# The keys' product of a recurrence level moved from VectorE to GpSimd

## The reference, cut to what matters

```python
log_f = jnp.logaddexp(jnp.log(lbf), jnp.log1p(-lbf) + jax.nn.log_sigmoid(f_logit))
k = -jnp.expm1(log_f)
bc = jnp.cumsum(log_f)                       # within a chunk
decay = jnp.exp(where(causal, diff of bc, -inf))
A = jnp.einsum('bhtk,bhsk,bhtsk->bhts', qx, kx, decay)
o_intra = A @ v;  o_inter = (q * exp(bc)) @ S
S_new = exp(b_last) * S + (k * exp(b_last - b)).T @ v
```

## Time and profile before

| | |
|---|---|
| median of 3 runs | 4003.78 us |
| the profiled execution's own time | 3998.87 us |
| its span | 3997.0 us |
| TensorE busy | 3660.4 us (92%) |
| VectorE busy | 2068.4 us (52%) |
| GpSimd busy | 1398.6 us (35%) |
| ScalarE busy | 863.5 us (22%) |
| mean granted clock of TensorE | 0.955 |

### The profile page before, as it was taken

How to read it: one execution, slowest core, us unless ns; L and a number is a source line. 1 busy time by engine, 2 the same in 40 slices (tenths; PEclk the granted TensorE clock), 3 DMA queues, 4 the chain that set the end, 5 groups by cost and what they waited for, 6 DMA issues and landing times. The chain is left out here.

```text
span 3997.0 us, 45908 instructions
## 1 busy us (share of the span) xinstructions
PE 3660.4 (92%) x18494; PEld 2943.3 (74%) x18494; DVE 2068.4 (52%) x3162; ACT 863.5 (22%) x1690; POOL 1398.6 (35%) x602
## 2 busy tenths in 40 slices
PE   7897878999999989978999799899999888899998
PEld 3683457888887879956888566788888566788886
DVE  5796453223337556674233367864243377853342
ACT  3213412110002243311100244431000343422001
POOL 2321034225555200005456222235445322245454
PEclk9998889999999999988999899999999899999999
DMA  5443312221113100013332131123332221123332
GB/s 169 148 148 138 121 42 64 64 64 58 53 40 98 53 14 1 2 63 94 96 100 90 54 85 49 48 62 101 96 95 79 74 67 48 53 79 92 98 93 76
DMA packets 400351, 306.81 MB, mean 77 GB/s; under 512 B 11228, under 2 KB 367782, under 8 KB 399559
## 3 DMA queue, kind: packets, MB, share of 16 engines
q1 hardware_dynamic: 398040, 303.37, 25.1%
q10 hardware_dynamic: 2095, 0.44, 0.1%
HBM read 297.48 MB, written 6.29 MB: 76 GB/s over the span
## 5 line engine op out<-in xcount | busy, mean ns | idle before, releaser
L422 POOL TENSOR_TENSOR low<-raw,high 128x1024 fp32r<-128x1024 f32 (+1 forms) x437 | 1060.6, 2427 | 1495.4 <-DVE high L346 1495.4
L487 PE MATMUL scores<-high 128*128 128x512 f32 (+1 forms) x1944 | 741.3, 381 | 85.4 <-POOL low L422 63.7
L487 PE MATMUL scores<-low,high 128*128 128x512 f32 (+1 forms) x1944 | 728.6, 375 | 0.0
L487 PE MATMUL scores<-high,low 128*128 128x512 f32 (+1 forms) x1944 | 726.6, 374 | 0.0
L346 DVE CAST high<-raw 128x1024 fp32r<-128x1024 f32 (+1 forms) x437 | 399.6, 915 | 501.7 <-PE scores L487 272.1
L487 PE MATMUL bank<-high 128*128 128x512 f32 (+1 forms) x1480 | 541.5, 366 | 0.2
L487 PE MATMUL bank<-low,high 128*128 128x512 f32 (+1 forms) x1480 | 538.8, 364 | 0.0
L487 PE MATMUL bank<-high,low 128*128 128x512 f32 (+1 forms) x1480 | 538.1, 364 | 0.0
L487 PEld LDWEIGHTS scores<-high 128*128 128x128 f32 x1944 | 377.2, 194 | 163.8 <-POOL low L422 68.0
L487 PEld LDWEIGHTS scores<-high,low 128*128 128x128 f32 x1944 | 375.1, 193 | 65.6
L487 PEld LDWEIGHTS scores<-low,high 128*128 128x128 f32 x1944 | 376.5, 194 | 62.5 <-issue 1.0
(11 more groups left out here) (628 smaller groups left out, 5396.0 us busy)
## 6 DMA issues: line engine op xcount, KB each, us to landing
raw<-in_mlp_w SPq DMA_DIRECT2D x128, 512.0 KB, 3.9
raw<-in_w_in SPq DMA_DIRECT2D x76, 512.0 KB, 3.9
ring<-in_ada_w SPq DMA_DIRECT2D x32, 1024.0 KB, 7.3
raw<-in_w_gate SPq DMA_DIRECT2D x44, 512.0 KB, 3.8
raw<-in_w_up SPq DMA_DIRECT2D x44, 512.0 KB, 3.8
raw<-in_w_down SPq DMA_DIRECT2D x40, 512.0 KB, 3.4
mix<-in_ada_w SPq DMA_DIRECT2D x16, 1024.0 KB, 7.0
raw<-in_od_w_in SPq DMA_DIRECT2D x29, 512.0 KB, 3.9
```

What stands on the lines that cost most here:

```text
L422: pool.tensor_tensor(tile(low, u), tile(raw, u), tile(high, u).bitcast(F32), ALU.subtract)\
L487: mm = pe.matmul(out(p), stationary, moving, start=(k0 + k == 0 and i == 0), stop=(k0 + k == job.kc - 1 and i == len(pairs) - 1))
```

## The change

The keys' product of each level is formed by GpSimd, after it has subtracted the weights of unit u+2 and before it goes on to unit u+1. It reads and writes the same tiles and raises the same semaphore; on GpSimd it waits for the pairing of three levels earlier and for the exponential.

```diff
@@ HgrnLevels.gpsimd @@
         if u == self.first - 1:
             pool.wait_ge(self.attention.kept, MH)
             pool.memset(self.attn, 0.0).then_inc(self.cleared, 1)
+        for a in self.at(u + 1):
+            hd, lv = self.units[a]
+            if lv < LEVELS:
+                if a >= self.RING:
+                    pool.wait_ge(self.paired, a - self.RING + 1)
+                pool.wait_ge(self.raised, self.decayed(a))
+                pool.tensor_tensor(self.ring(self.ke, a), self.k[:, hd, :], self.ring(self.e, a), ALU.mult)\
+                    .then_inc(self.keys_decayed, 1)
@@ HgrnLevels.vector @@
                 dve.wait_ge(self.raised, self.decayed(a))
                 dve.tensor_tensor(self.ring(self.qe, a), self.q[:, hd, :], self.ring(self.e, a), ALU.mult)\
                     .then_inc(self.queries_decayed, 1)
-                dve.tensor_tensor(self.ring(self.ke, a), self.k[:, hd, :], self.ring(self.e, a), ALU.mult)\
-                    .then_inc(self.keys_decayed, 1)
```

## The result

The changed kernel took 4024.18 us (median of 5 runs, 4019.0 to 4029.31) against 4001.8 us (median of 5, 4000.95 to 4003.97) for the kernel before: 1.0053 times as long, 95% interval 1.0038 to 1.0067. It is 22.4 us slower; 21.8 us and 4025 us had been forecast.

The account below looks back on a forecast made before the run. VectorE's loop was taken to bound the levels' stage; trip terms summed to 10.9 us per layer, 21.8 us for two, giving 4025 us from a median of 4003.8, range 4008 to 4040.

Parts of the forecast that it names:

- Who sets the stage: Levels' stage of either layer: VectorE's loop sets the pace, working or waiting 135.9 of 141.1 us; TensorE follows.
- The plain trip: VectorE's loop: cast done at T + 3.90 to 3.98, not T + 3.01 (T: first exponential ready); 0.9 us per trip.
- The price of a key that waited: GpSimd's keys' product after waiting for VectorE: 1.18 us in place of 1.26.
- Unit 31: Trip with the cumulated sum, which could be held up differently: left at 0.9 us, between 0.6 and 0.9.
- Units 33 and 34: GpSimd runs `low` and `ya_low` before unit 33's keys, delaying the next subtractions and products: 1.5 us for both trips.
- Unit 35: VectorE afterwards waits 3.5 us for ScalarE's gate function, which does not depend on the keys: 0 us.
- Unit 36: VectorE's 0.5 us of wait for TensorE is there to be used up: 0.4 us.
- The signs: Profile after: one query per trip 1.3 us or more, longer casts, GpSimd some 95 us busier, stage about 152 us.
- That the engines run side by side: Rival: GpSimd's multiply does not exclude VectorE's, about 10 trips per layer gain 0.6 us, 3992 us; 7%.
- That it is hidden: Rival: TensorE sets the pace and VectorE's waits have slack, so no change, 4004 us; 10%.
- The costlier rival: Rival: TensorE's clock falls more often or each handover costs, 31 us and more, 4035 to 4042 us; 13%.
- The 115 ns: Skill's figure for a blocked engine's restart; at four handovers, 0.46 us per trip, estimate 4035 us; not used.

Follow-up runs that it names:

- the run of the memsets: Changed kernel with the keys' product left out and GpSimd writing zeros twice into each key tile instead, same waits: 3996.1 us, stage 137.9 us.

## Why the prediction was right, point by point

The starts of the first query of each trip, read off VectorE's timeline of both kernels (first layer), give the price of every trip:

```
unit            29    30    31    32    33+34  35    36    37    38    39    40    41    42    sum
before       10.62 11.64 12.24  7.52  20.81  12.62  9.20 10.28  7.80  7.53  8.73  8.76 10.32
changed      11.61 12.55 12.84  8.47  22.36  12.62 10.09 11.28  8.72  8.52  9.64  9.74 11.31
difference    0.99  0.91  0.60  0.95   1.55   0     0.89  1.00  0.92  0.99  0.91  0.98  0.99  11.7
forecast      0.9   0.9   0.9   0.9    1.5    0     0.4   0.9   0.9   0.9   0.9   0.9   0.9   10.9
```

(The last is to the first step of the states. The columns of this table are trips as VectorE runs them; 34's query is left out, since it meets a key in the changed kernel.)

*Who sets the stage.* VectorE's loop: shown by the run without keys, in which 12 of the 14 trips get shorter when VectorE loses two products in each, nine of them by the products' own 0.6 us.

*The plain trip.* 0.96 us as a mean of nine (29, 30, 32 and 37 to 42) for 0.9. The order of the handovers came out as written, the first query, a key, the second query, a key, the cast. The price of a key that waited, 1.18 us, was near (T + 2.31 for T + 2.25 when the cast is issued).

*Unit 31.* I named 0.6 to 0.9 and took 0.9; it was 0.60. Before, VectorE's line 3212 started late, 0.44 us of it for ScalarE, and GpSimd's `low` had gone ahead of it at 2526.43; the cumulated sum then ran undisturbed. In the changed kernel line 3212 no longer waits, goes ahead of `low` (from 2537.58), and the sum is held in its place, which is cheaper: after the end of `low` VectorE has one instruction left in place of two. Before, then changed:

```profile
2526.79 2.55 DVE L3212 SCALAR_TENSOR_TENSOR x_all<-b,x_all 128x512 f32<-128x512 f32 x1 [0.44 <-ACT x_all L3225]
2529.38 1.22 DVE L3214 TENSOR_TENSOR_SCAN b<-restart,x_all 128x512 f32<-128x512 f32 x1
...
2537.42 0.68 DVE L3212 SCALAR_TENSOR_TENSOR x_all<-b,x_all 128x512 f32<-128x512 f32 x1
2538.14 3.27 DVE L3214 TENSOR_TENSOR_SCAN b<-restart,x_all 128x512 f32<-128x512 f32 x1
```

In the changed kernel all eight of these sums are held:

```profile
L3214 DVE TENSOR_TENSOR_SCAN b<-restart,x_all x8: 3273/3286/3307, 2401.2 to 3422.9; 128x512 f32<-128x512 f32 x8
```

*Units 33 and 34.* 1.55 us for 1.5. VectorE's and GpSimd's timelines show the walk: both queries undisturbed, the cast at T + 4.2 held until GpSimd's `ya_low` is through, GpSimd's two keys and `low` after it, and the two subtractions and the two queries stretched between them.

```profile
2554.77 0.69 DVE L3333 TENSOR_TENSOR work<-q,work 128x512 f32<-128x512 f32 x1 [0.83 <-ACT work L3355]
2555.96 0.69 DVE L3333 TENSOR_TENSOR work<-q,work 128x512 f32<-128x512 f32 x1 [0.49 <-ACT work L3355]
...
2558.96 2.83 DVE L346 CAST high<-raw 128x1024 fp32r<-128x1024 f32 x1
...
2564.00 3.47 DVE L3324 TENSOR_TENSOR work<-b 128x512 f32<-128x512 f32 x2
2567.39 3.49 DVE L3333 TENSOR_TENSOR work<-q,work 128x512 f32<-128x512 f32 x2
```
```profile
2557.87 3.38 POOL L370 TENSOR_TENSOR ya_low<-ya,ya_high 128x1024 fp32r<-128x1024 f32 x1 [5.07 <-DVE ya_high L359]
2561.21 2.94 POOL L3297 TENSOR_TENSOR work<-f,work 128x512 f32<-128x512 f32 x2
2564.11 2.81 POOL L422 TENSOR_TENSOR low<-raw,high 128x1024 fp32r<-128x1024 f32 x1
```

*Unit 35.* 0 for 0: the wait for ScalarE's gate function shrank from 3.5 to 2.5 us and took it all in.

*Unit 36.* The term mis-sized most: 0.89 for 0.4. I counted VectorE's 0.5 us of wait for TensorE as there to be used up. But TensorE's product in that unit took 7.3 us in place of 6.4, at the lower of its two clock levels for longer, so the wait was still 0.4 us. The first of its 24 products start some 0.43 us apart, the later ones 0.23, and the slow stretch lasts 3.1 us in place of 1.4. The granted clock over that product, before and after, in the columns of the earlier trace rows:

```profile
2574.10:2580.60 6.50, 6.50 (x29) 5.36 (x28) 3.94 (x7) 5.43 (x14) 0.97 (x1) 0.88 0.00 1
```
```profile
2587.40:2594.80 7.40, 7.40 (x29) 6.04 (x28) 4.45 (x5) 5.44 (x14) 4.37 (x3) 0.76 0.00 0
```

In the second layer the same trip went from 9.29 to 9.73 us, 0.44, which is what I had counted on; that is the difference between the layers' 11.7 and 11.2. The slack is there, then, but it is TensorE's, and its clock moves it.

*The terms together.* Nine plain trips +0.5, unit 31 -0.3, 33 and 34 +0.05, unit 36 +0.5: 11.7 for 10.9 in the first layer. With the second layer's 11.2 that is 22.9 us; the medians differ by 22.4, against the 21.8 forecast. The errors partly cancel, but the largest is 0.5 us.

*The signs.* The stage came to 151.85 us for "about 152", the cast, where it stands directly behind the queries, to 1.75 us and more for "1.5 us and more", GpSimd's busy time to 95.4 us more over both layers for "some 95", its products to 1.73 us as a mean for 1.8. One sign was missed in size: the second query of a trip lasts 1.20 us, not 1.3 or more. Its record begins only with the second exponential, at T + 1.19, and ends at T + 2.4.

*The rivals.* That the engines run side by side fell with the plain trip and with the run of the memsets, which is what side by side looks like. That it is hidden fell with the stage. The costlier rival did not happen: TensorE's mean clock in the stage did fall, to 0.91, but in the trips above that shows only as 0.5 us in one trip of one layer.

*The 115 ns.* The Trainium skill ("SBUF — State Buffer", section "A bandwidth-pool intuition that's wrong (but worth ruling out)") gives "blocked until DVE-end + ~115 ns" for a DMA whose descriptors GpSimd has to write. Carried over to the four handovers of a trip, as the prediction's estimate by that page did, it would make a plain trip cost 0.90 + 0.46 = 1.4 us. It cost 0.96; the traces here show no such addition between compute instructions.

## What to carry to other kernels

When an instruction is moved from VectorE to GpSimd, add up how long the two engines exclude each other, not how long each is busy: here 1.2 us of VectorE's time per trip was traded for 2.4 us of GpSimd's in which VectorE's two-input products and casts could not run, and the trip came out 0.96 us longer. In these runs GpSimd's work was free only beside VectorE's masked copies out of PSUM, beside VectorE's waits, or, next to a two-input product, when it only wrote. Look first at the order inside the loop: with the subtractions ahead of the cast the same instructions, none moved to another engine, gave 31 us.

## What the runs showed of the hardware that was not expected

- The two engines hand over without a loss that these rows would show. A VectorE instruction that has stood waiting lets the next one start 0.47 us after GpSimd's end, 0.13 less than undisturbed (in the changed kernel 0.46: 2561.25 to 2561.71 around the held cast of unit 33). In the rows read here, whoever has waited goes before the other's next instruction.
- What excludes what, by these runs: GpSimd's one-input copy and a two-input VectorE product exclude each other (the copy takes 1.14 us for 0.61); GpSimd's memset and the same product do not (0.53 and 0.69 us side by side); memset and VectorE's fp32 cast of SBUF do (1.06 for 0.69 us); a masked copy of data in PSUM runs beside a GpSimd subtraction unhindered (1.57 us for two). A one-input VectorE instruction can be held too: line 3204, a multiply and add of one SBUF tile by columns, never takes less than 2.58 us in the kernel before, each time beside a GpSimd `low` after whose end it ends some 0.25 us later, where line 3203 on the same shape takes 0.48.
